# Five pieces of the conditioning weights are fetched in the opening stage, and ScalarE rounds the rows of the convolution

## The chip, the cores and the metric

The kernel runs on one core of one Trainium2 chip. The metric is the device time of one execution in microseconds (us), lower is better. It is one long program of about 137,000 instructions, written with explicit semaphores, one queue of instructions for each engine: TensorE (PE), VectorE (DVE), ScalarE (ACT), GpSimd (POOL) and SyncE (SP), which here only issues transfers.

## The reference, cut to what matters

One inference step of a network of four layers over 128 context tokens and 1024 latent tokens of 1024 channels, in float32. The mixers are RWKV-7, attention, a gated short convolution, and RWKV-7 again. Each layer is wrapped like this:

```python
def sublayer(x, cond, p, i, mixer_fn):
    ada = jax.nn.silu(cond) @ p['w_ada'][i] + p['b_ada'][i]     # 1024 -> 3072, two rows of cond
    shift, scale, gate = jnp.split(ada[:, None, :], 3, axis=-1)
    h = rmsnorm(x, p['norm_pre'][i]) * (1.0 + scale) + shift
    m, extra = mixer_fn(h)
    return x + gate * rmsnorm(m, p['norm_post'][i]), extra

def conv_mixer(h, p, j):
    proj = h @ p['conv_w_in'][j]                                # 1024 -> 4096
    bg, cg, u, g = jnp.split(proj, 4, axis=-1)
    ...
```

The change touches the product with `w_ada` (its fetching) and the rows `h` that enter `conv_w_in`.

## The kernel before

Activations lie in SBUF as 128 partitions (channels of a block) by 8 blocks by 1152 tokens. The scratch memory `arena` is four such arrays, `big[0]` to `big[3]`; `g.x` is a fifth. Tokens are worked in three chunks of 384, each a PSUM bank. The phases run one after the other and each ends in a barrier of all engines: opening, then for each layer projection, scan or attention, and a boundary with the output projection.

**Conditioning.** `w_ada` of the four layers is six groups of eight pieces, 1 MB each (128 partitions x 2048). A piece is multiplied with the two conditioning columns by `ada_products` (line 167). Group 0 is worked in the opening phase (`phase_open`, all eight pieces in `big[2]` and `big[3]`). Groups 1, 2 and 3, that is 24 pieces numbered 0 to 23, are worked in the projection phase of layer 0, and groups 4 and 5 in the convolution.

**Opening phase.** SP issues everything at once: x, ones, eight pieces, constants, and the first two weight slabs of the next phase. PE sums the squares, then takes the eight products (`rows_mm` counts the last). ACT copies four rows of the result, PE turns them, DVE has meanwhile scaled the eight blocks of x (line 305, `tmp_ok`), and then DVE and ACT apply scale and shift (lines 315 and 275). SP waits for its last transfers before the barrier.

**Projection phase of layer 0** (`phase_rwkv_project`). The 24 pieces pass through two buffers of 1 MB in `g.x[:, 4:8]`. PE runs `lora_down(0)`, `lora_down(1)` and `first_keys`, each of eight steps k = 0 to 7 of six fp32 matmul instructions (lines 588 and 626); behind each step `ada_between(n, k)` puts piece 2 + 8n + k, and pieces 0 and 1 come ahead of `lora_down(0)`. After the last step of `lora_down(0)` PE raises `proj_done` to 1, after that of `lora_down(1)` to 2, and only then comes the piece of k = 7. The rows of `lora_down(0)` are made in `big[2]` by ACT (line 798) and DVE (line 895), those of `lora_down(1)` in `big[3]`.

SP issues in program order and waits in that order too: `pieces(0, 12)`, then `slab(2)`, which waits for `proj_done` 1, then `pieces(12, 20)`, then `slab(3)`, which waits for `proj_done` 2, then `pieces(20, 24)`. A piece p of 2 or more waits until PE has used piece p - 2 (`piece_mm`).

When a group of eight is complete, ACT copies its rows out (line 183), PE turns them (`ada_columns`, behind step k = 2 of the next group of steps), and DVE adds the bias; DVE does that for group 1 behind its fifth row of the keys.

**Convolution** (`phase_conv`). Every matmul there is split in three with operands rounded to fp32r: high by high, high by low, low by high, in 32 slabs of 8 steps k of nine matmuls (line 370). DVE makes all operands: it rounds slab 0 (line 339) and subtracts (line 349), then for each of eight rows rounds (line 339) and subtracts (line 357), then does slab 1. PE's first slab waits for each row in turn. ACT loads a table at the start and has nothing to do until the first slab is done.

Of the kernel before, what the change touches and what calls it, by code (L numbers as in the profile page):

```python
# [22 lines left out]
NB = D // P  # L23
# [11 lines left out]
WSLOTS = 2  # L35
# [124 lines left out]
ADA_TILES = 4  # L160
# [3 lines left out]
def ada_products(pe, g, piece, bank, k):  # L164

    for t in range(ADA_TILES):
        mm = pe.matmul(g.ps[32 * t:32 * t + 2, bank, :], g.silu[:, 2 * k:2 * k + 2], piece[:, t * 512:(t + 1) * 512],
                       start=k == 0, stop=k == NB - 1)
    return mm
# [41 lines left out]
def phase_open(nc, g, layer):  # L211

    io = g.io
# [4 lines left out]
    size = ADA_TILES * 512  # L218
    pieces = [rest[:, k * size:(k + 1) * size] for k in range(NB)]
# [6 lines left out]
    with ExitStack() as ctx:  # L226
        sem = Sems(nc, ctx)
        cond_in, ident_in, ones_in, chan_in, next_in, set_ok, sig_ok, silu_ok = sem(
            "cond_in", "ident_in", "ones_in", "chan_in", "next_in", "set_ok", "sig_ok", "silu_ok")
# [7 lines left out]
        @block.sync  # L237
        def _(sp):
            sp.dma_start(cond, io["cond"]).then_inc(cond_in, 16)
            n = NB // X_PARTS  # L240
            for i in range(X_PARTS):
                sp.dma_start(g.x[:, n * i:n * i + n, :], io["x"][:, n * i:n * i + n, :]).then_inc(x_in[i], 16)
            sp.dma_start(g.ones[:, :], io["ones"]).then_inc(ones_in, 16)
            for k in range(NB):
                sp.dma_start(pieces[k], io["w_ada"][0, k]).then_inc(piece_in[k], 16)
            sp.dma_start(g.ident[:, :], io["ident"]).then_inc(ident_in, 16)
            sp.dma_start(g.chan[:, :], io["chan"]).then_inc(chan_in, 16)
            sp.dma_start(g.head_ones[:, :], io["head_ones"]).then_inc(next_in, 16)
            for s in range(WSLOTS):
                sp.dma_start(g.slab[:, s, :], io["w"][mixer_slabs(layer) + s]).then_inc(next_in, 16)  # L250
            sp.wait_ge(next_in, 16 * (WSLOTS + 1))

        @block.scalar
        def _(act):
# [82 lines left out]
def take_high(nc, dst, src):  # L337

    return nc.vector.tensor_copy(dst, src)
# [9 lines left out]
    nc.vector.tensor_tensor(g.slab_r[:, n % WSLOTS], g.slab[:, n % WSLOTS], g.stage_r[:, n % WSLOTS, 0:D], op=ALU.subtract).then_inc(low_ok, 1)  # L349


def split_rows(nc, g, dve, high, low, rows_high_ok, rows_ok):

    for k in range(NB):
        take_high(nc, g.big_r[high][:, k, :], g.big[low][:, k, :]).then_inc(rows_high_ok, 1)
        dve.wait_ge(rows_high_ok, k + 1)
        nc.vector.tensor_tensor(g.big_r[low][:, k, :], g.big[low][:, k, :], g.big_r[high][:, k, :], op=ALU.subtract).then_inc(rows_ok, 1)  # L357


def multiply_split(pe, g, high, low, slot, bank, done, rows_ok=None, late=None):  # L360

    w_high, w_low = g.stage_r[:, slot, 0:D], g.slab_r[:, slot]
# [36 lines left out]


ADA_WITH = ((1, 2, 3), (), (4, 5), ())


RWKV_MATS = (("decay", 4, 1), ("rate", 5, 1), ("key", 1, NB), ("receptance", 0, NB), ("value", 2, NB), ("gate", 3, NB))
# [2 lines left out]
def phase_rwkv_project(nc, g, layer, j):  # L407
# [17 lines left out]
    ada_in = ADA_WITH[layer]  # L425
# [31 lines left out]
    with ExitStack() as ctx:  # L457
# [19 lines left out]
        def _(sp):  # L477
# [49 lines left out]

            def pieces(first, last):
                for p in range(first, min(last, n_pieces)):
                    if p >= 2:  # L530
                        sp.wait_ge(piece_mm, p - 1)
                    sp.dma_start(piece[p % 2], g.io["w_ada"][ada_in[p // NB], p % NB]).then_inc(piece_in[p % 2], 16)

            pieces(0, 12)
            slab(2)
            pieces(12, 20)
            slab(3)
# [45 lines left out]
        def _(pe):  # L583
# [13 lines left out]
            def ada_piece(p):  # L597
                i = p // NB
                if p >= n_pieces:
                    return  # L600
                pe.wait_ge(piece_in[p % 2], 16 * (p // 2 + 1))
                if p % NB == 0 and i >= 2:
                    pe.wait_ge(cols_sb, i - 1)
                mm = ada_products(pe, g, piece[p % 2], ada_bank(i), p % NB)
                mm.then_inc(piece_mm, 1)

            def ada_columns(i):
# [3 lines left out]
                ada_turned(pe, g, ada_row[i % 2], ada_bank(i)).then_inc(cols_mm, 1)  # L611

            def ada_between(n, k):
                if n < 2 or k < 6:
                    ada_piece(2 + NB * n + k)
                if n and k == 2:
                    ada_columns(n - 1)

# [74 lines left out]
                bank_free(("sum", b, c))  # L693
                pe.matmul(g.ps[:, bank(("sum", b, c)), 0:CW], g.head_ones[:, :], prod[b % 2][:, chunk(c)], start=True, stop=True).then_inc(sum_mm, 1)

            ada_piece(0)
            ada_piece(1)
            lora_down(0)
            lora_down(1)
            first_keys()  # L700
# [20 lines left out]
        def _(act):  # L721
# [69 lines left out]
            def scaled_rows(m, k):  # L791
                r = RWKV_MATS[m][1]
                if m == 2:
                    if k < NB - 1:
                        act.wait_ge(rows_free, k + 1)
                    else:
                        act.wait_ge(proj_done, 2)
                A.activation((lora_xs[0], lora_xs[1], low)[m][:, k, :], h[:, k, :], ACT.Copy, scale=rest_mu[:, 8 * r + k:8 * r + k + 1]).then_inc(pre_ok, 1)

            def ada_row_copies(i):  # L800
# [73 lines left out]
        def _(dve):  # L874
# [116 lines left out]

            for b in range(NB):
                from_scaled(2, b, xs_ok)
                if b == 4:
                    ada_columns(0)
            high_slab_of(KEY + 1)
            for b in range(NB):
# [1279 lines left out]
def phase_conv(nc, g):  # L2277
# [11 lines left out]
    with ExitStack() as ctx:  # L2289
# [53 lines left out]

        @block.scalar
        def _(act):
            act.preload_act_table_set(SIGMOID)
            for b in range(NB):
                act.wait_ge(proj_done, 4 * b + 1)
                if b:
                    act.wait_ge(u_ok, b)  # L2350
                A.copy(as3(cs), slot_view(g.ps[:, 0:3, :])).then_inc(c_ok, 1)
                act.wait_ge(proj_done, 4 * b + 4)
                if b:
                    act.wait_ge(silu_ok, b)
                A.activation(as3(sig), slot_view(g.ps[:, 3:6, :]), ACT.Sigmoid).then_inc(sig_ok, 1)
                if b in (3, 5):
                    i = (b - 3) // 2
                    act.wait_ge(zero_ok, 1)
                    act.wait_ge(piece_mm, NB * (i + 1))
                    ada_rows(nc, g, ada_row[i], ada_bank(i), rows_sb)  # L2360
            act.preload_act_table_set(LN_EXP)

        @block.vector
        def _(dve):
            def next_slab(n):
                if n < 4 * NB:
                    split_slab(nc, g, dve, n, slab_in, proj_done, high_ok, low_ok)

            next_slab(0)
            split_rows(nc, g, dve, H_HIGH, H_LOW, rows_high_ok, rows_ok)  # L2370
            next_slab(1)
            for b in range(NB):
                dve.wait_ge(proj_done, 4 * b + 1)
                next_slab(4 * b + 2)
                w = lambda i: ch(g, "conv_w", 8 * i + b)
                dve.wait_ge(proj_done, 4 * b + 2)
                dve.wait_ge(c_ok, b + 1)
                V.tensor_tensor(as3(uu), slot_view(g.ps[:, 3:6, :]), as3(cs), op=ALU.mult).then_inc(evacuated, 1)
                next_slab(4 * b + 3)
                dve.wait_ge(evacuated, 3 * b + 1)  # L2380
                V.tensor_scalar(cv, uu, w(1), ch(g, "conv_b", b), ALU.mult, ALU.add).then_inc(w1_ok, 1)
                dve.wait_ge(w1_ok, b + 1)
                for _, a0, a1 in token_ranges():
                    V.scalar_tensor_tensor(cv[:, a0 + 1:a1], uu[:, a0:a1 - 1], w(0), cv[:, a0 + 1:a1], op0=ALU.mult, op1=ALU.add).then_inc(w0_ok, 1)
                dve.wait_ge(w0_ok, 2 * b + 2)
                for i, (_, a0, a1) in enumerate(token_ranges()):
                    V.scalar_tensor_tensor(cv[:, a0:a1 - 1], uu[:, a0 + 1:a1], w(2), cv[:, a0:a1 - 1], op0=ALU.mult, op1=ALU.add).then_inc(w2_ok, 1)
                dve.wait_ge(w2_ok, 2 * b + 2)
                V.tensor_copy(g.flag[:, 2:3], g.flag[:, 1:2]).then_inc(u_ok, 1)
                dve.wait_ge(proj_done, 4 * b + 3)  # L2390
                V.tensor_tensor(as3(cv), slot_view(g.ps[:, 0:3, :]), as3(cv), op=ALU.mult).then_inc(evacuated, 1)
                next_slab(4 * b + 4)
                dve.wait_ge(evacuated, 3 * b + 2)
                dve.wait_ge(sig_ok, b + 1)
                V.tensor_tensor(as3(gg), slot_view(g.ps[:, 3:6, :]), as3(sig), op=ALU.mult).then_inc(evacuated, 1)
                next_slab(4 * b + 5)
                dve.wait_ge(evacuated, 3 * b + 3)
                dve.wait_ge(u_ok, b + 1)
                V.tensor_tensor(og[:, b, :], cv, gg, op=ALU.mult).then_inc(silu_ok, 1)
                dve.wait_ge(silu_ok, b + 1)  # L2400
                if b in (4, 6):
                    i = b // 2 - 2
                    dve.wait_ge(cols_mm, i + 1)
                    ada_biased(nc, g, ada_in[i], ada_bank(i), cols_sb)
            dve.wait_ge(cols_sb, len(ada_in))
            ada_gate(nc, g, 2, vec_ok)
            ada_scale(nc, g, 3, vec_ok)
            ada_gate(nc, g, 3, vec_ok)
            dve.wait_ge(vec_ok, 3)
# [445 lines left out]
```

## Time and profile before

| | |
|---|---|
| time, median of 3 runs | 4689.62 us (4684.68 to 4690.49) |
| the profiled execution's own time | 4690.08 us |
| its span | 4688.3 us |
| PE, DVE, ACT busy | 91%, 58%, 40% |
| mean granted TensorE clock | 0.968 of full |

The span is the time from the first to the last instruction; a DMA issue, a wait and a branch are not counted as busy. SPq is the queue of SP, in which DMA issues stand. A wait that was released by an engine is shown behind the arrow in brackets.

### The profile page before, as it was taken

How to read it: one execution, taken by the hardware profiler on the slowest of the kernel's cores; microseconds unless marked ns; L12 is line 12 of the kernel's file. 1: busy time of each engine (PE TensorE's matmuls, PEld its weight loads, DVE VectorE, ACT ScalarE, POOL GpSimd, SP SyncE). 2: the span in 40 equal slices, each digit the busy share in tenths (PEclk: the TensorE clock that was granted, in tenths of full speed). 3: DMA queues.
4: the chain of work that ended last, by engine and by line, in shares of the span. 5: the costliest groups of instructions: out<-in, count | busy, mean ns of one | idle time of the engine just before them, and what ended most of it. 6: DMA issues, size and time to landing. Idle time of an engine off the chain costs nothing. (4 is left out here: it accounts for less than half of the span.)

```text
span 4688.3 us, 137401 instructions
## 1 busy us (share of the span) xinstructions
PE 4258.9 (91%) x61184; PEld 3665.6 (78%) x61184; DVE 2696.7 (58%) x4665; ACT 1887.8 (40%) x3496; POOL 4.6 (0%) x10
## 2 busy tenths in 40 slices
PE   6999979999997899999998999889999789999978
PEld 2888768888885799766668899877988678888858
DVE  5433547777775654355556433466425577777755
ACT  5333225545554432355554000154332245555542
POOL 0000000000000000000000000000000000000000
PEclk8999989999999999899999999999999899999989
DMA  7444773333325132100000221112446733333341
GB/s 294 150 123 123 223 225 87 98 83 97 87 80 192 63 84 56 51 1 2 1 10 28 95 95 68 57 52 82 117 139 195 236 110 89 98 85 96 85 183 63
DMA packets 542442, 480.77 MB, mean 103 GB/s; under 512 B 29344, under 2 KB 500640, under 8 KB 534176
## 3 DMA queue, kind: packets, MB, share of 16 engines
q1 hardware_dynamic: 411040, 405.91, 27.3%
q10 hardware_dynamic: 130816, 66.07, 5.2%
q8 instruction: 487, 7.98, 0.7%
q14 instruction: 99, 0.81, 0.1%
HBM read 337.94 MB, written 128.71 MB: 100 GB/s over the span
## 5 line engine op out<-in xcount | busy, mean ns | idle before, releaser
L647 PE MATMUL ps<-big_r,stage_r 128*128 128x384 f32 x2976 | 641.3, 350 | 19.1 <-DVE big_r L908 17.7
L647 PEld LDWEIGHTS ps<-big_r,stage_r 128*128 128x128 f32 x2976 | 522.6, 190 | 75.7 <-issue 27.0
L2508 PE MATMUL ps<-big_r,w_out 128*128 128x384 f32 x2304 | 417.8, 341 | 36.5 <-DVE w_out L2624 36.2
L2508 PEld LDWEIGHTS ps<-big_r,w_out 128*128 128x128 f32 x2304 | 407.7, 191 | 44.9 <-DVE w_out L2624 39.2
L647 PE MATMUL ps<-big_r,w_slab_r 128*128 128x384 f32 x1488 | 341.4, 337 | 0.0
L370 PE MATMUL ps<-big_r,stage_r 128*128 128x384 f32 x1536 | 311.7, 337 | 13.2 <-DVE big_r L357 13.2
L2230 DVE TENSOR_REDUCE extra<-ps 128x1 f32<-128x1152 f32 (+1 forms) x144 | 177.6, 1234 | 205.0 <-PE ps L2135 205.0
L370 PEld LDWEIGHTS ps<-big_r,stage_r 128*128 128x128 f32 x1536 | 270.7, 189 | 27.7 <-issue 26.7
L1491 ACT COPY arena<-ps 128x512 f32<-128x512 f32 x288 | 168.9, 587 | 253.4 <-PE ps L1294 252.9
L647 PEld LDWEIGHTS ps<-big_r,w_slab_r 128*128 128x128 f32 x1488 | 268.2, 189 | 0.0
L1645 DVE COPY_PREDICATED arena<-arena,ps 128x128 f32<-128x128 uint32 x720 | 192.9, 325 | 116.6 <-PE ps L1282 115.5
L1518 ACT COPY arena<-ps 128x256 f32<-128x256 f32 x360 | 136.4, 379 | 273.5 <-PE ps L1305 222.3
L764 ACT ACTIVATE x_resid<-ps,chan 128x384 f32<-128x384 f32 x192 | 101.1, 578 | 308.7 <-PE ps L685 224.4
L2156 PE MATMUL ps<-ident,arena 128*128 128x128 f32 x1168 | 189.4, 286 | 27.5 <-ACT arena L2215 20.9
L1282 PE MATMUL ps<-arena 64*64 64x32 f32 x7680 | 164.1, 222 | 55.1 <-ACT arena L1491 48.1
L1294 PE MATMUL ps<-arena 64*64 64x64 f32 x9216 | 202.5, 224 | 7.2 <-DVE arena L1645 2.5
L1247 PE MATMUL ps<-arena 64*128 64x128 f32 x2304 | 172.3, 289 | 38.7 <-DVE arena L1617 25.4
L1282 PEld LDWEIGHTS ps<-arena 64*64 64x64 f32 x7680 | 138.1, 135 | 77.8 <-ACT arena L1491 61.8
L1247 PEld LDWEIGHTS ps<-arena 64*128 64x128 f32 x2304 | 144.3, 191 | 67.9 <-issue 41.5
L1294 PEld LDWEIGHTS ps<-arena 64*64 64x64 f32 x9216 | 165.3, 135 | 39.1 <-issue 16.0
L1305 PE MATMUL ps<-ident,arena 128*128 128x128 f32 x1152 | 189.8, 287 | 3.5 <-issue 3.5
L2205 ACT ACTIVATE arena<-ps,extra 128x1152 f32<-128x1152 f32 (+1 forms) x144 | 162.1, 1126 | 74.1 <-DVE extra L2230 70.0
(259 smaller groups left out, 8087.5 us busy)
## 6 DMA issues: line engine op xcount, KB each, us to landing
w_slab<-in_w SPq DMA_DIRECT2D x138, 512.0 KB, 3.7
scan_in<-x_resid ACTq DMA_DIRECT2D x112, 576.0 KB, 5.9
arena<-scan_in SPq DMA_DIRECT2D x144, 320.0 KB, 3.8
arena<-scan_in SPq DMA_DIRECT2D x288, 128.0 KB, 3.8
arena<-scan_in SPq DMA_DIRECT2D x48, 576.0 KB, 7.5
arena<-scan_in SPq DMA_DIRECT2D x144, 192.0 KB, 4.0
arena<-in_w_ada SPq DMA_DIRECT2D x24, 1024.0 KB, 5.8
x_resid<-in_w_ada SPq DMA_DIRECT2D x24, 1024.0 KB, 4.9
```

What stands on the lines that cost most here:

```text
L370: mm = pe.matmul(g.ps[:, bank + c, 0:CW], w[:, k * P:(k + 1) * P], x[:, k, c * CW:(c + 1) * CW], start=k == i == 0, stop=k == NB - 1 and i ...
L647: mm = pe.matmul(g.ps[:, 3 * s + c, 0:CW], w[:, k * P:(k + 1) * P], x[:, k, chunk(c)], start=k == i == 0, stop=k == NB - 1 and i == 2)
L1247: mm = pe.matmul(strided(ps, (3 + h) * 512 + u * P, (1, P)), strided(bk[q % 2], u * 256 + t * P, (1, P), rows=HALVES[h]), strided(ar[q % 4 ...
L1282: mm = pe.matmul(strided(ps, p * 512 + u * 32, (1, 32), rows=HALVES[h]), strided(gr[q % 3], (1 - p) * 1024 + h * 512 + u * P, (1, HD), row ...
L1294: mm = pe.matmul(strided(ps, h * 512 + (2 * d + s) * HD, (1, HD), rows=HALVES[p]), strided(xt[q % 2], lx(d, p, s), (1, HD), rows=HALVES[h] ...
L1305: mm = pe.transpose(strided(ps, 2 * 512 + lx(d, 0, s), (P, 2), (1, HD)), strided(x, (2 * d + s) * P, (1, P)), g.ident[:, :])
L1491: A.copy(strided(x, 0, (HD, 2), (P, 4), (1, HD)), strided(ps, 0, (512, 2), (HD, 4), (1, HD))).then_inc(xa_ok, 1)
L1645: V.copy_predicated(strided(wk(k), p * P, (256 + n, 2), (2 * n, HD // n), (1, n)), bits(strided(level_mask, (k - 1) * P, (HD, 2), (n, HD / ...
L2156: mm = pe.transpose(g.ps[:, bank, i * P:(i + 1) * P], prob[n % 2][h][:, (3 * k + i) * P:(3 * k + i + 1) * P], g.ident[:, :])
L2205: A.activation(prob[n % 2][h][:, 0:width(n)], scored(n, h), ACT.Exp, bias=nmax[n % 2][h], accum_out=rsum[n % 2][h]).then_inc(exp_ok, 1)
L2230: V.tensor_reduce(nmax[n % 2][h], scored(n, h), mybir.AxisListType.X, ALU.max, negate=True).then_inc(max_ok, 1)
L2508: mm = pe.matmul(g.ps[:, bank(i, b), 0:wide[i]], w[:, b, k * P:(k + 1) * P], r, start=k == j == 0, stop=k == NB - 1 and j == 2)
```

## The change

Five of the 24 pieces are now issued in the opening phase: pieces 2, 3 and 4 into `big[3]` once its eight products are done, pieces 0 and 1 into `g.x[:, 4:8]` once the blocks of x there have been scaled. The opening phase ends when they have landed. The projection phase multiplies them ahead of `lora_down(0)`; the pieces between the steps are now numbered 5 + 8n + k, without the bound on n and k. The lists that SP walks become `pieces(5, 12)`, `slab(2)`, `pieces(12, 20)`, `slab(3)`, `pieces(20, 24)`, and the wait of each is counted from the two buffers anew. ACT waits for the five products before it writes rows of `lora_down(1)` into `big[3]`. DVE takes the columns of group 1 behind its second row of the keys and not its fifth. In the convolution ACT rounds the eight rows ahead of its table load, and DVE only subtracts. The last layer's projection has no pieces and keeps its order.

```diff
@@ phase_open, sync
-            sp.wait_ge(next_in, 16 * (WSLOTS + 1))
+            sp.wait_ge(rows_mm, 1)
+            for p in range(2, ADA_EARLY):
+                sp.dma_start(early_piece(g, p), io["w_ada"][ADA_WITH[layer][0], p]).then_inc(next_in, 16)
+            for p in range(2):
+                sp.wait_ge(tmp_ok, (6, NB)[p])
+                sp.dma_start(early_piece(g, p), io["w_ada"][ADA_WITH[layer][0], p]).then_inc(next_in, 16)
+            sp.wait_ge(next_in, 16 * (WSLOTS + 1 + ADA_EARLY))
@@
+ADA_EARLY = 5
+def early_piece(g, p):
+    size = ADA_TILES * 512
+    if p < 2:
+        return g.x[:, 4:8, :].rearrange("p b t -> p (b t)")[:, p * size:(p + 1) * size]
+    return g.big[3].rearrange("p b t -> p (b t)")[:, (p - 2) * size:(p - 1) * size]
@@ phase_rwkv_project, sync
             def pieces(first, last):
                 for p in range(first, min(last, n_pieces)):
-                    if p >= 2:
-                        sp.wait_ge(piece_mm, p - 1)
-                    sp.dma_start(piece[p % 2], g.io["w_ada"][ada_in[p // NB], p % NB]).then_inc(piece_in[p % 2], 16)
-            pieces(0, 12)
+                    i = p - ADA_EARLY
+                    sp.wait_ge(piece_mm, i + 1 if i < 2 else p - 1)
+                    sp.dma_start(piece[i % 2], g.io["w_ada"][ada_in[p // NB], p % NB]).then_inc(piece_in[i % 2], 16)
+            pieces(ADA_EARLY, 12)
             slab(2)
             pieces(12, 20)
             slab(3)
@@ phase_rwkv_project, tensor
-                pe.wait_ge(piece_in[p % 2], 16 * (p // 2 + 1))
+                r = p - ADA_EARLY
+                if r >= 0:
+                    pe.wait_ge(piece_in[r % 2], 16 * (r // 2 + 1))
...
-                mm = ada_products(pe, g, piece[p % 2], ada_bank(i), p % NB)
+                mm = ada_products(pe, g, piece[r % 2] if r >= 0 else early_piece(g, p), ada_bank(i), p % NB)
...
             def ada_between(n, k):
-                if n < 2 or k < 6:
-                    ada_piece(2 + NB * n + k)
+                ada_piece(ADA_EARLY + NB * n + k)
...
-            ada_piece(0)
-            ada_piece(1)
+            for p in range(ADA_EARLY):
+                ada_piece(p)
@@ phase_rwkv_project, scalar
+                if m == 1 and k == 0 and ada_in:
+                    act.wait_ge(piece_mm, ADA_EARLY)
@@ phase_rwkv_project, vector
-                if b == 4:
+                if b == 1:
                     ada_columns(0)
@@ phase_conv, scalar
+            for k in range(NB):
+                A.copy(g.big_r[H_HIGH][:, k, :], g.big[H_LOW][:, k, :]).then_inc(rows_high_ok, 1)
             act.preload_act_table_set(SIGMOID)
@@ phase_conv, vector
-            split_rows(nc, g, dve, H_HIGH, H_LOW, rows_high_ok, rows_ok)
+            for k in range(NB):
+                dve.wait_ge(rows_high_ok, k + 1)
+                V.tensor_tensor(g.big_r[H_LOW][:, k, :], g.big[H_LOW][:, k, :], g.big_r[H_HIGH][:, k, :], op=ALU.subtract).then_inc(rows_ok, 1)
```

## Rows read from the trace of the kernel before

**Rows 1.** The page, its first part: busy us, share, instructions of each engine.

```profile
PE 4258.9 (91%) x61184; PEld 3665.6 (78%) x61184; DVE 2696.7 (58%) x4665; ACT 1887.8 (40%) x3496; POOL 4.6 (0%) x10
```

**Rows 2.** Timeline of the opening phase: start, duration, engine, line.

```profile
33.40 7.05 PE L167 MATMUL ps<-arena,silu 128*2 128x512 f32 x64
37.29 10.24 DVE L305 TENSOR_TENSOR arena<-x_resid,extra 128x1152 f32<-128x1152 f32 x8 [2.42 <-ACT extra L267]
47.88 6.17 ACT L275 ACTIVATE arena<-arena,ada 128x128 f32<-128x128 f32 x8 [4.93 <-DVE ada L200]
55.10 17.71 SPq L532 DMA_DIRECT2D x_resid<-in_w_ada  x6
```

**Rows 3.** Timeline of the projection phase's start, all engines.

```profile
56.64 18.45 ACT L798 ACTIVATE arena<-arena,stage 128x1152 f32<-128x1152 f32 x16
58.04 1.42 DVE L895 SCALAR_TENSOR_TENSOR arena<-arena,stage 128x1152 f32<-128x1152 f32 x1 [0.46 <-ACT arena L798]
60.01 1.89 PE L167 MATMUL ps<-x_resid,silu 128*2 128x512 f32 x8 [16.29 <-DMA x_resid<-in_w_ada]
64.30 4.05 PE L588 MATMUL ps<-arena,w_slab 128*128 128x384 f32 x6
68.28 1.04 PE L167 MATMUL ps<-x_resid,silu 128*2 128x512 f32 x8
69.25 2.20 PE L588 MATMUL ps<-arena,w_slab 128*128 128x384 f32 x6
71.38 1.04 PE L167 MATMUL ps<-x_resid,silu 128*2 128x512 f32 x8
```

**Rows 4.** Waits between 64 and 142 us: total, times, longest.

```profile
PE ps L167 <- DMA x_resid<-in_w_ada: 2.5, 5, 0.6
```

**Rows 5.** Waits of SP's queue from 55 to 145 us.

```profile
SPq L532 <- PE ps L167: 67.9, 22, 6.0
```

**Rows 6.** Timeline of SP at slab(2), and of PE at the first split slab.

```profile
88.00 4.15 SPq L532 DMA_DIRECT2D x_resid<-in_w_ada  x2
92.19 0.43 SPq L485 DMA_DIRECT2D w_slab<-in_w  x1
141.75 1.50 PE L647 MATMUL ps<-big_r,stage_r 128*128 128x384 f32 x6
```

**Rows 7.** Line 532's transfers; then those issued from 91 to 101 us, median to landing.

```profile
DMA to landing us min/median/max: 4.7/4.9/7.0
w_slab<-in_w SPq DMA_DIRECT2D x1, 512.0 KB, 5.9
```

**Rows 8.** Windows: us, PE, PEld, DVE, ACT, POOL busy (instructions), PEclk, DMA, GB/s.

```profile
24.00:27.00 3.00, 3.00 (x11) 1.81 (x10) 0.00 (x0) 2.22 (x2) 0.00 (x0) 1.00 1.02 423
47.60:54.00 6.40, 0.00 (x0) 0.00 (x0) 4.22 (x10) 6.12 (x8) 0.00 (x0) 0.50 0.00 0
2563.30:2570.00 6.70, 4.25 (x7) 2.31 (x8) 6.53 (x13) 4.49 (x8) 0.00 (x0) 0.50 0.00 0
2587.70:2593.80 6.10, 6.07 (x19) 6.10 (x20) 6.00 (x7) 0.00 (x0) 0.00 (x0) 0.50 0.00 0
```

**Rows 9.** Timeline of PE before the convolution: a wait inside the boundary phase.

```profile
2565.75 8.79 PE L2536 MATMUL ps<-arena,ones 128*128 128x384 f32 x16 [6.16 <-ACT arena L2573]
```

**Rows 10.** Timeline of the convolution's start.

```profile
2585.44 0.75 DVE L339 CAST big_r<-arena 128x1152 fp32r<-128x1152 f32 x1
2586.23 1.36 DVE L357 TENSOR_TENSOR big_r<-arena,big_r 128x1152 fp32r<-128x1152 f32 x1
2587.73 2.26 PE L370 MATMUL ps<-big_r,stage_r 128*128 128x384 f32 x6 [13.19 <-DVE big_r L357]
2604.46 1.20 PE L370 MATMUL ps<-big_r,stage_r 128*128 128x384 f32 x6
2606.02 1.20 PE L370 MATMUL ps<-big_r,stage_r 128*128 128x384 f32 x6
```

**Rows 11.** Line 724: ACT's rounding of a row; duration ns min/median/max.

```profile
L724 ACT CAST big_r<-arena x64: 1134/1155/1167, 98.2 to 3563.0; 128x1152 fp32r<-128x1152 f32 x64
```

More of the change, by code:

```diff
@@ L349, in split_slab @@
     nc.vector.tensor_tensor(g.slab_r[:, n % WSLOTS], g.slab[:, n % WSLOTS], g.stage_r[:, n % WSLOTS, 0:D], op=ALU.subtract).then_inc(low_ok, 1)
[L352 to L357, printed above, removed]
 def multiply_split(pe, g, high, low, slot, bank, done, rows_ok=None, late=None):
```

## The prediction

> **What bounds the kernel now.** I read the page first: PE is busy 91% of the span [rows 1], so an edit counts only where it changes when PE works. The change touches two stretches, and each was read in the timeline, then in the waits. In the opening, the eight products end at 40.45 (33.40 + 7.05), DVE's scaling of x ends at 47.53, ACT's last shift at 54.05, and the next phase begins at 55.10 [rows 2]. PE has no work until the first piece, issued at 55.10, lands at 60.01, and `lora_down(0)` starts at 64.30 [rows 3]. From there to 141.75, where the first split slab starts [rows 6], PE is the bound: it waits 2.5 us in all for pieces, in 5 waits [rows 4], while SP is the one that waits for PE, 67.9 us in 22 waits [rows 5]. One step costs 2.13 us (69.25 to 71.38), and one piece 0.97 us (68.28 to 69.25) [rows 3]. In the convolution PE's first slab starts when DVE's first row is ready, 2587.73 [rows 10].
>
> **The pieces fetched ahead: when the opening ends.** Between 47.6 and 54 no transfer runs [rows 8], so the fetch lies beside other work, but it is 5 MB in a short time. A piece alone takes 4.9 us from issue to landing [rows 7]. The full stream is 423 GB/s [rows 8], by which 1.05 MB takes 2.5 us; the other 2.4 us are fixed. SP is released at 40.5 for three pieces. Pieces 0 and 1 are released after six and eight of DVE's scalings (10.24 / 8 = 1.28 us each), at 45.0 and 47.5, while earlier ones still stream. So the fifth lands at 40.6 + 2.4 + 5 x 2.5 = 55.5, against ACT's end at 54.05 today: SP becomes the last one at the barrier and the next phase starts 1.4 us later, at 56.5. Bounds: 0, if the stream is as fast as the cover allows, and 2.8 if each of the last two takes 0.7 longer. I take 1.4.
>
> **The start of the projection phase.** PE now has five pieces at once. The clock stands at 0.50 (1.2 GHz) in the idle stretch. After PE resumed elsewhere it stayed there for 4.3 us (2565.75 to 2570.0) [rows 8, 9] and 6.1 us (2587.7 to 2593.8) [rows 8], and here for some 8 us, with gaps between the products (60.01 to about 68.2, where the short groups begin) [rows 3]. For unbroken work I take 5.2, between the first two. A piece at the slow clock costs 1.75 us (twice 7.05 / 8 = 0.88, and 1.89 for one alone). In 5.2 us go three pieces, two more take 1.8: `lora_down(0)` starts at 56.5 + 7.0 = 63.5, 0.8 us before today. Its first step no longer runs slow (4.05 against 2.20 [rows 3]), 1.9 us more. Gain 2.7, the later start paid. Bounds: 3.2, if the clock rises after 4.3 us; -1.6, if products with two columns of weights don't raise it (five slow pieces end at 65.2, then 5.2 us of steps run slow and lose 2.6, against 1.9 today).
>
> **The steps.** Three pieces fewer lie between the steps: 3 x 0.97 = 2.9 us. Of the 2.5 us of small waits [rows 4] I leave 0.5, gain 2.0 (0 to 2.5). DVE's first row is ready at 59.46 today, so about 60.9, ahead of 63.5. ACT's new wait for five products costs nothing: it comes to `lora_down(1)`'s rows half way through its 18.45 us, at 67 [rows 3], with PE done at 63.5. DVE's columns behind its second row: the piece that needs them is now that behind step 3 of `lora_down(1)`, one step (2.13 us) after the turn; the add of some 0.2 us fits. Were it left behind the fifth row, the engines would block each other. Together these stretches give 2.7 + 2.9 + 2.0 = 7.6 us.
>
> **What SP's order does to the shifted pieces.** This is the step that decides. Behind step k = 7 of `lora_down(0)` stood piece 9; now piece 12 stands there. But SP issues `pieces(5, 12)`, then `slab(2)`, then piece 12, and `slab(2)` waits for `proj_done` 1, which PE raises with that very step 7. Today piece 12 has until k = 2 of `lora_down(1)`. Now PE comes to it at once, with its transfer not yet issued, though its buffer was free since step 5. The same holds for piece 20, behind step 7 of `lora_down(1)`, and `slab(3)`. How long: today piece 11 is issued at about 91.8 (the last of the two issues that end at 92.15) and the slab at 92.19, and the slab lands 5.9 us later, so 1.5 MB takes 6.3 us from the first issue [rows 6, 7]; slab and piece in the other order are the same 1.5 MB. I take 6.3 for each stall, 12.6 for both. Bounds for one: 5.3 (a lone piece's 4.9 and the slab's issue of 0.43) and 8.8 (piece 13, issued behind it, streams beside it and ends first, 2.5 more). Behind PE nothing else is late: rows, ACT's copies and slabs get longer cover.
>
> **The clock after a stall.** In the boundary phase PE waited 6.16 us, and worked at 0.50 after it until 2570 [rows 8, 9]. So each stall should be followed by about 5.2 us of work at 1.2 GHz, of which half is lost: 2.6 each, 5.2 for both. Bounds: 0 and 6.2. The Trainium skill (TensorE: Matmul & The Clock Gate, "HAM oscillation — how this bites in real kernels") warns of this: when matmuls wait for a transfer between groups, the clock falls back and the next group starts cold. By that rule the two stalls cost 17.8 us, without it 12.6. The trace agrees with the rule where it shows a 6.16 us wait.
>
> Sum in this stretch: 12.6 + 5.2 - 7.6 = +10.2 us, and PE stays the bound behind 141.75, so all of it passes on.
>
> **The convolution.** DVE's roundings go (0.75 each), ACT's take 1.155 [rows 11], start at the phase's start and run ahead of DVE, whose subtractions come each 1.3 us behind slab 0. The first row is ready 0.79 us sooner (2585.44 against 2586.23). After that the rows of today hardly hold PE up: it takes 16.73 us for the slab (2587.73 to 2604.46) [rows 10], and its own work is 6.1 us at the slow clock (two steps, at twice the 1.56 us from 2604.46 to 2606.02), six steps at 1.56 and one piece of 0.97, together 16.4 to 16.5 [rows 8, 10]. So 0.2 us of small waits go too. ACT's table load moves behind its roundings, which end 8 x 1.155 = 9.2 us after the phase's start, and nothing asks for ACT before PE's first slab ends, 21.7 us after it. Gain 1.0, bounds 0.4 (the clock rises no sooner, so half of 0.79 is given back, and no wait goes) and 1.3.
>
> Total: +9.2 us on the profiled execution's own 4690.08, which stands 0.5 above the median: 4699.
>
> **Rivals.** (A) The clock doesn't fall in the stalls. Then 12.6 - 7.6 - 1.0 = +4.0, 4694. For it: a stall of 6.3 us has one match in the rows, and the place of that one is another phase. Against it: that one match ran at 0.50 behind the wait [rows 8, 9]. (B) Not slower: the fetched pieces give SP its lead and PE finds piece 12 and 20 ready, so that the gains alone stand: -7.6 - 1.0 = -8.6, 4681.5. It holds if the slab's wait is over before PE reaches step 7's piece; the change is no loss from a stall of (7.6 + 1.0) / 2 = 4.3 us each downwards if the clock holds, and from 4.3 - 2.6 = 1.7 us if it falls. For it speaks that SP is ahead of PE today. Against it: the release of the slab is the end of the step directly before the piece, and the 2.4 us of a transfer that are no streaming can't be hidden behind anything there. The Trainium skill (DMA: Bandwidth & Descriptors, "Rules for kernel authors") says to issue early and wait late, so that the fixed cost overlaps; by it the change would be all gain. The same page ("Anatomy of one DMA") says that a semaphore wait is done by the issuing sequencer ahead of dispatch, by which what is behind the slab's wait isn't early. (C) Stalls near their upper bound, with piece 13 in the same stream, or products that don't raise the clock: 2 x 1.5 more, or 4.3 more: 4702 to 4703.
>
> **How the numbers follow.** My forecast 0.68 (its own range 4695 to 4702), A 0.10, B 0.05, C 0.17. A difference under 0.2%, 9.4 us, can't be told from none here. The forecast lies at that bound, +9.2. I give a little under half of it, and nearly all of C, to slower; A and the rest of the forecast to no change; B sits at the edge of faster. Faster 0.04, same 0.48, slower 0.48. The range reaches into A and C, with both ends of the clock's cost: 4691 to 4704.
>
> **What would show it.** In the trace after: the last instruction of the opening waits for SP and the next phase starts at about 56.5; `lora_down(0)` starts at 63 to 64; two waits of PE on `in_w_ada` of about 6.3 us, right behind the last steps of `lora_down(0)` (near 87) and `lora_down(1)` (near 121), with the slab's issue at their start; a clock of 0.50 behind each; the first split slab at about 152. In the convolution PE starts 4.2 us after the phase and not 5.0. I am wrong if PE's longest wait for a piece stays under 2 us, or if the clock holds at 1.00 through both, or if the opening's end moves by over 3 us.

## The result, and the profile after

The changed kernel takes 4700.34 us (median of 12 runs, 4687.86 to 4707.96) against 4690.18 of before on the same chip. Ratio 1.0021, 95% interval 1.0012 to 1.0029: slower by 0.21%, or 9.8 us (the two medians are 10.2 apart). One of the 12 runs of before took 13653.26 us, and the ratio leaves it out. The prediction was 4699. The profiled execution spans 4698.2 us, 9.9 more than before.

The timeline of PE and SP in the opening and the projection phase of the changed kernel, in order of time (start, duration, engine, line; line 253 and 256 are the fetches, 539 the other pieces, 492 the slabs, 595 and 634 the steps, 655 the split slabs):

```profile
40.73 1.28 SPq L253 DMA_DIRECT2D arena<-in_w_ada  x3
45.24 2.86 SPq L256 DMA_DIRECT2D x_resid<-in_w_ada  x2
48.09 6.17 ACT L281 ACTIVATE arena<-arena,ada 128x128 f32<-128x128 f32 x8 [4.93 <-DVE ada L200]
56.61 3.60 PE L167 MATMUL ps<-x_resid,silu 128*2 128x512 f32 x16 [12.67 <-PEq L151]
59.97 3.53 PE L167 MATMUL ps<-arena,silu 128*2 128x512 f32 x24
63.44 2.20 PE L595 MATMUL ps<-arena,w_slab 128*128 128x384 f32 x6
65.57 1.04 PE L167 MATMUL ps<-x_resid,silu 128*2 128x512 f32 x8
...
85.84 2.20 PE L595 MATMUL ps<-arena,w_slab 128*128 128x384 f32 x6
88.07 0.33 SPq L492 DMA_DIRECT2D w_slab<-in_w  x1
88.44 25.45 SPq L539 DMA_DIRECT2D x_resid<-in_w_ada  x8
94.23 1.88 PE L167 MATMUL ps<-x_resid,silu 128*2 128x512 f32 x8 [6.19 <-DMA x_resid<-in_w_ada]
96.05 3.69 PE L595 MATMUL ps<-arena,w_slab 128*128 128x384 f32 x6
...
122.56 0.33 SPq L492 DMA_DIRECT2D w_slab<-in_w  x1
128.59 1.88 PE L167 MATMUL ps<-x_resid,silu 128*2 128x512 f32 x8 [6.06 <-DMA x_resid<-in_w_ada]
130.41 3.58 PE L634 MATMUL ps<-arena,w_slab 128*128 128x384 f32 x6
...
150.97 1.50 PE L655 MATMUL ps<-big_r,stage_r 128*128 128x384 f32 x6
```

Read it against [rows 2, 3, 6]. ACT ends the opening's work at 54.26, and the next phase starts at 56.6 and not 55.1. `lora_down(0)` starts at 63.44, 0.86 us sooner than before and at the fast clock. Then come the two stalls, each with the slab's issue at its start: the last step of `lora_down(0)` ends at 88.0, SP issues the slab at 88.07 and piece 12 at 88.44, and PE has it at 94.23 (the slab itself landed 3.6 us after its issue, at 91.7). The second stall is the same, from 122.53 to 128.59. The first split slab starts at 150.97 against 141.75: +9.22 us.

SP's own waits from 55 to 152 us in the changed kernel (what waited, for whom: total, times, longest) show its waits ahead of the slabs, for the last step, and what held the end of the opening:

```profile
SPq L492 <- PE ps L595: 17.2, 2, 8.6
SPq L226 <- DMA x_resid<-in_w_ada: 7.4, 1, 7.4
```

And the windows of the changed kernel (columns as in [rows 8]) show the clock in the first products, and ahead of, in and behind the stalls:

```profile
56.70:61.00 4.30, 4.30 (x24) 0.78 (x23) 3.80 (x6) 4.29 (x6) 0.82 (x1) 0.50 0.34 86
61.40:61.80 0.40, 0.40 (x8) 0.10 (x4) 0.40 (x1) 0.40 (x2) 0.00 (x0) 0.83 1.01 430
88.10:91.80 3.70, 0.00 (x0) 0.00 (x0) 2.98 (x3) 1.11 (x1) 0.00 (x0) 1.00 0.76 270
92.00:92.50 0.50, 0.00 (x0) 0.00 (x0) 0.00 (x0) 0.00 (x0) 0.00 (x0) 0.76 0.83 344
92.00:98.50 6.50, 4.27 (x12) 1.62 (x13) 0.00 (x0) 0.00 (x0) 0.00 (x0) 0.52 0.72 281
99.00:99.20 0.20, 0.20 (x1) 0.10 (x1) 0.00 (x0) 0.00 (x0) 0.00 (x0) 0.79 1.16 492
126.00:132.60 6.60, 4.01 (x12) 1.39 (x13) 1.92 (x2) 3.78 (x6) 0.00 (x0) 0.53 0.80 300
```

A value between 0.50 (1.2 GHz) and 1.00 (2.4 GHz) means that the change lies within the window. In the products the clock rose at about 61.6. It fell within the first stall, at about 92.2, and rose again at about 99.1, so that PE worked at 1.2 GHz for 4.8 us behind it (94.23 to 99.1). In the second stall it fell at about 126.4, and PE worked slowly for 4.6 us.

In the convolution (phase start at 2593.17), the rows answering to [rows 10, 11]:

```profile
2593.18 8.54 ACT L2357 CAST big_r<-arena 128x1152 fp32r<-128x1152 f32 x8 [1.01 <-PEq L151]
2595.84 10.23 DVE L2384 TENSOR_TENSOR big_r<-arena,big_r 128x1152 fp32r<-128x1152 f32 x8
2597.34 2.26 PE L368 MATMUL ps<-big_r,stage_r 128*128 128x384 f32 x6 [12.39 <-DVE big_r L2384]
2612.80 1.20 PE L368 MATMUL ps<-big_r,stage_r 128*128 128x384 f32 x6
```

The clock rises there at about 2601.05, 3.7 us after PE's first matmul (6.2 in the kernel before):

```profile
2600.90:2601.30 0.40, 0.40 (x3) 0.40 (x3) 0.40 (x2) 0.40 (x1) 0.00 (x0) 0.81 0.00 0
```

PE starts 4.17 us after the phase (4.96 before), and its second slab 19.63 us after it (21.69 before, 2604.46 - 2582.77): 2.06 us won, where 1.0 was forecast.

### The profile page after: what moved, and what is told of

Same layout as the page of the kernel before. It is cut to its first block and busy times, and to the rows that moved or that the text cites. A ratio compares the mean times of both kernels' runs of the same rounds, so it can differ in the third digit from the quotient of the medians.

```text
span 4698.2 us, 137401 instructions
## 1 busy us (share of the span) xinstructions
PE 4261.7 (91%) x61184; PEld 3666.5 (78%) x61184; DVE 2690.5 (57%) x4657; ACT 1895.6 (40%) x3504; POOL 4.6 (0%) x10
```

## The experiments

In all of them "first split slab" is the start of the first of the split slabs, the end of the stretch that the change touches. Two executions with the same code up to there, in which the clock rises at the same place, agree there to 0.6 us (141.75 in the kernel before, 141.12 in the kernel with the convolution's part alone); a rise at another place was worth 1.9 us in one of those below. Whole runs of one kernel differ by 14 to 25 us.

**SP's order.** The slabs are moved behind three more pieces:

```diff
-            pieces(ADA_EARLY, 12)
+            pieces(ADA_EARLY, 15)
             slab(2)
-            pieces(12, 20)
+            pieces(15, 23)
             slab(3)
-            pieces(20, 24)
+            pieces(23, 24)
```

> The changed kernel with SP's lists as pieces(5, 15), slab(2), pieces(15, 23), slab(3), pieces(23, 24): piece 12 and piece 20 no longer stand behind a slab that waits for the step just ahead of them. My theory (the order behind the slabs costs two stalls of 6.2 and 6.1 us and the slow clock after them 2.5 us each, 17 us in all): both stalls go, small waits of about 1 us come back, the clock stays at 1.00, the first split slab starts at about 135 us and not 150.97, the time is 16 us under the changed kernel's and 7 under that of before, ratio to before 0.9985. Rival (the transfers themselves are late, since five fetched pieces move the stream closer to its limit): the waits go to other pieces, the first split slab stays near 148 to 151, ratio 1.001 to 1.002.

Measured: ratio 0.9984 (0.9974 to 0.9993). PE's waits for pieces are small again; these are the three over 0.2 us and the first split slab:

```profile
97.54 1.04 PE L167 MATMUL ps<-x_resid,silu 128*2 128x512 f32 x8 [0.32 <-DMA x_resid<-in_w_ada]
110.81 1.04 PE L167 MATMUL ps<-x_resid,silu 128*2 128x512 f32 x8 [0.21 <-DMA x_resid<-in_w_ada]
123.72 1.04 PE L167 MATMUL ps<-x_resid,silu 128*2 128x512 f32 x8 [0.42 <-DMA x_resid<-in_w_ada]
134.56 1.50 PE L655 MATMUL ps<-big_r,stage_r 128*128 128x384 f32 x6
```

16.4 us sooner than in the changed kernel (150.97), with the same transfers, bytes and instructions. The change of order alone turns +9.8 us into about -7.5 (interval of the ratio: -12 to -3). The rival, transfers that are late by themselves, is out: the waits that come back are 1.2 us in 4 waits.

**Stall and clock apart.** Eight matmuls that nobody reads are put ahead of PE's wait for pieces 12 and 20 (for piece 20 they wait until ACT has copied the bank out):

```diff
+                if p in (12, 20):
+                    if p == 20:
+                        pe.wait_ge(copied, 1)
+                    for _ in range(8):
+                        pe.matmul(g.ps[:, 3 if p == 12 else 0, 0:CW], g.ones[:, :], g.chan[:, 0:CW], start=True, stop=True)
```

> The changed kernel, with eight matmuls more (ones by constants, into a PSUM bank that nobody reads before it is started anew) ahead of PE's wait for piece 12 and for piece 20: 5.7 us of work inside each stall. It does 16 matmuls that the result doesn't need. My theory (stall and clock are two costs): the transfers land as before, the waits that are left are about 0.5 us, the clock stays at 1.00, and the first split slab starts 4.9 us sooner, at 146. Ratio to before about 1.001. Rival (the steps behind the stalls are slow for another reason, or the clock falls all the same): first split slab at 151, ratio 1.002.

Measured: ratio 1.0011 (1.0001 to 1.0022). PE around piece 12, and the first split slab:

```profile
88.73 5.32 PE L613 MATMUL ps<-chan,ones 128*128 128x384 f32 x16
94.95 1.04 PE L167 MATMUL ps<-x_resid,silu 128*2 128x512 f32 x8 [0.90 <-DMA x_resid<-in_w_ada]
95.92 2.20 PE L595 MATMUL ps<-arena,w_slab 128*128 128x384 f32 x6
146.75 1.50 PE L660 MATMUL ps<-big_r,stage_r 128*128 128x384 f32 x6
```

The step behind the piece takes 2.20 us and not 3.69. In this execution the projection phase began 0.9 us later, so from its first product (57.50) to the first split slab it is 89.25 us, against 94.36 (150.97 - 56.61): 5.1 us less. The piece and the step behind each stall now take 3.10 us, against 5.44 and 5.32: 4.6 of the 5.1 us are the clock, and PE got them back by doing more work. The rest is other small waits for pieces, 0.8 less, and a start that took 0.2 longer. The waits that are left behind the added matmuls are 0.90 and 1.07 us, where 0.5 was forecast, and 146.75 is 0.75 behind the forecast, about as much as the late start. The whole-time ratios of this one and the changed kernel overlap; the trace decides it.

**The order alone, in the kernel before.**

```diff
-            pieces(0, 12)
+            pieces(0, 9)
             slab(2)
-            pieces(12, 20)
+            pieces(9, 17)
             slab(3)
-            pieces(20, 24)
+            pieces(17, 24)
```

> The kernel before, with one thing of the changed one: SP's lists are pieces(0, 9), slab(2), pieces(9, 17), slab(3), pieces(17, 24), so that the piece behind the last step of lora_down(0) and of lora_down(1) is issued behind a slab that waits for that step. Nothing is fetched ahead. My theory: two stalls of 6.2 us and 2.5 us of slow clock behind each, less about 1.7 of the small waits of before (those of the pieces beside the slabs); the first split slab starts at 141.75 + 15.5 = 157, ratio to before 1.0033. Rival (in the kernel before there is slack in SP's order that takes it up): under 5 us.

Measured: ratio 1.0032 (1.0020 to 1.0044). Its two stalls, the step behind the first, and its first split slab:

```profile
94.96 1.88 PE L167 MATMUL ps<-x_resid,silu 128*2 128x512 f32 x8 [6.22 <-DMA x_resid<-in_w_ada]
96.77 2.99 PE L588 MATMUL ps<-arena,w_slab 128*128 128x384 f32 x6
128.12 1.89 PE L167 MATMUL ps<-x_resid,silu 128*2 128x512 f32 x8 [6.25 <-DMA x_resid<-in_w_ada]
153.90 1.50 PE L647 MATMUL ps<-big_r,stage_r 128*128 128x384 f32 x6
```

The same stalls with nothing fetched ahead. The first split slab came 12.2 us later, not 15.5; in this execution the clock had risen by the first step (64.36, 2.20 us and not 4.05), which is 1.9 of the 3.3 us missing. Most of the rest is in the rows too: the slow clock behind the stalls cost 1.6 us (94.96 to 99.69, against 3.10) and 2.1 (128.12 to 133.34), 3.7 in all where 5.0 was forecast, and of the 2.5 us of small waits only 0.3 are left, where 0.8 was forecast.

**Two pieces ahead and not five** (`ADA_EARLY = 2`, the lists as they are, so that the numbering and the order of the kernel before come back).

> The changed kernel with two pieces fetched in the opening and not five (those in x, none in the scratch memory); SP's lists are pieces(2, 12), slab(2), pieces(12, 20), slab(3), pieces(20, 24), as in the kernel before, and the pieces between the steps are numbered as there. My theory: the fetch lands by 52.5 us, ahead of ACT's end at 54, so the next phase starts at 55.1; PE takes two pieces at the slow clock to 58.7, waits for DVE's first row at 59.5, and starts lora_down(0) at 59.6, the first step or two at the slow clock; no stall behind the slabs. The first split slab starts 3 to 5 us sooner than before, at 137 to 139; ratio to before 0.999. Rival (fetching ahead gives nothing since DVE's rows bound the start of lora_down(0)): DVE makes a row each 2.8 us against PE's 3.1, so that under 1 us is won.

Measured: ratio 0.9985 (0.9975 to 0.9995), first split slab at 138.42. The start:

```profile
55.26 3.59 PE L167 MATMUL ps<-x_resid,silu 128*2 128x512 f32 x16 [11.37 <-PEq L151]
59.63 4.21 PE L595 MATMUL ps<-arena,w_slab 128*128 128x384 f32 x6 [0.78 <-DVE arena L905]
```

The barrier isn't later, PE waits 0.78 us for DVE's first row, and the first step runs at the slow clock (4.21 us against 2.20). Of the 4.7 us by which it starts sooner, 3.3 arrive; of the difference, 0.9 are small waits for pieces (3.4 us in 6 waits, against 2.5 in 5). Whole times of this and the kernel with the moved order can't be told apart, though the first split slab is 3.9 us apart.

**Four pieces ahead, moved order** (`ADA_EARLY = 4`; `pieces(4, 14)`, `slab(2)`, `pieces(14, 22)`, `slab(3)`, `pieces(22, 24)`).

> The kernel with the moved order, and four pieces fetched in the opening and not five; SP's lists are pieces(4, 14), slab(2), pieces(14, 22), slab(3), pieces(22, 24). My theory (the fifth piece's landing, and nothing else, held the opening's end): the four land by 53, the next phase starts at 55.1 to 55.3 and not 56.6, lora_down(0) at 61.5 to 62.5, one piece more lies between the steps, and the first split slab starts 0.5 to 1.5 us sooner than with five, at 133 to 134. Ratio to before 0.998. Rival (the barrier is late for another reason, such as pieces 0 and 1 being released late by VectorE): the phase starts at 56.6 again, and the first split slab at 135.5.

Measured: ratio 0.9985 (0.9976 to 0.9994), the phase starts at 55.44, `lora_down(0)` at 60.39, the first split slab at 132.63, 1.9 us sooner than with five. So the landing of the fifth piece did hold the barrier. The four landed at about 54.3 and not by 53, just ahead of ACT's end at 54.4. `lora_down(0)` and the first split slab were earlier than I expected (61.5 to 62.5, and 133 to 134), since the clock rose while the products ran: two took 3.27 us, the next two 1.89. The rise came 2.8 us after the first product, against 5.0 with five pieces. PE does half as much at the slow clock, so by my estimate half of that difference, 1.1 of the 1.9 us, is the clock's, so what four pieces win over five is nearer to 0.8 us.

```profile
55.48 3.27 PE L167 MATMUL ps<-x_resid,silu 128*2 128x512 f32 x16 [11.41 <-PEq L151]
58.57 1.89 PE L167 MATMUL ps<-arena,silu 128*2 128x512 f32 x16
60.39 0.91 PE L595 MATMUL ps<-arena,w_slab 128*128 128x384 f32 x2
```

**The convolution alone**, the kernel before with the convolution's part of the diff.

> The kernel before with the convolution's part of the change alone: ScalarE rounds the eight rows, VectorE subtracts. My theory: PE starts its first slab 4.2 us after the phase's start and not 5.0, and finishes it 1.0 us sooner if the clock takes as long to rise, that is 20.6 to 20.8 us after the phase's start against 21.69 in the kernel before; the 19.63 of the changed kernel had the clock rise 3.3 us after PE's start against 6.1. Ratio to before 0.9998, not to be told from 1. Rival (the shorter row time itself gives the 2 us): 19.6 us after the phase's start with the clock rising as late as before.

Measured: ratio 0.9999 (0.9990 to 1.0008), not to be told from 1, as expected. PE starts 4.17 us after the phase; the second slab comes 19.69 us after it, better than the 20.6 to 20.8 forecast for a late rise, but the clock rose early here too, 3.8 us after PE's start. The rival (the shorter rows give the 2 us by themselves, with a late rise too) fails on the kernel with four pieces ahead, where the rise was late and the second slab came at 20.71. What shows the rest is the old split with an early rise, which the third experiment (the order alone) happens to hold. Its convolution starts at 2592.43, its PE at 2597.39, and the clock rises 3 us later. Its windows, with one of the kernel with four pieces ahead at the end:

```profile
2597.40:2600.30 2.90, 2.90 (x9) 2.90 (x10) 2.83 (x4) 0.00 (x0) 0.00 (x0) 0.50 0.00 0
2600.50:2612.00 11.50, 10.87 (x63) 9.10 (x61) 11.33 (x12) 0.00 (x0) 0.00 (x0) 1.00 0.01 1
2580.50:2580.90 0.40, 0.40 (x3) 0.40 (x3) 0.40 (x2) 0.00 (x0) 0.00 (x0) 0.70 0.00 0
```

And its steps, in order of time:

```profile
2605.55 1.33 PE L370 MATMUL ps<-big_r,stage_r 128*128 128x384 f32 x6 [0.20 <-DVE big_r L357]
2607.62 1.31 PE L370 MATMUL ps<-big_r,stage_r 128*128 128x384 f32 x6 [0.20 <-DVE big_r L357]
2609.68 1.32 PE L370 MATMUL ps<-big_r,stage_r 128*128 128x384 f32 x6 [0.23 <-DVE big_r L357]
2614.12 1.20 PE L370 MATMUL ps<-big_r,stage_r 128*128 128x384 f32 x6
```

PE now stands 2.07 us apart from step to step, which is the pace of DVE's rounding and subtracting, and the second slab starts 21.69 us after the phase, the same as with the late rise. The table (us; the rise from PE's first matmul, the second slab from the phase's start):

| execution | rows made by | clock rises after PE's start | second slab |
|---|---|---|---|
| before | DVE | 6.2 | 21.69 |
| order alone | DVE | 3.0 | 21.69 |
| four ahead | ACT and DVE | 6.1 | 20.71 |
| convolution alone | ACT and DVE | 3.8 | 19.69 |
| changed kernel | ACT and DVE | 3.7 | 19.63 |
| order moved, kept warm, two ahead | ACT and DVE | 3.5 to 3.6 | 19.56 to 19.60 |

The expectation has 3.3 for the changed kernel; the window above gives 3.7. So the new split is worth 1.0 us with a late rise and 2.0 with an early one. In the old one DVE's pace holds PE as soon as the clock is up, and an earlier rise bought nothing.

**Clock kept up at both starts.** The kernel with four pieces ahead, with matmuls that nobody reads (14 behind the turn in the opening, 3 ahead of the convolution's first slab):

```diff
             ada_turned(pe, g, rows, COLS).then_inc(cols_mm, 1)
+            pe.wait_ge(chan_in, 16)
+            for _ in range(14):
+                pe.matmul(g.ps[:, 5, 0:CW], g.ones[:, :], g.chan[:, 0:CW], start=True, stop=True)
...
+            for _ in range(3):
+                pe.matmul(g.ps[:, 7, 0:CW], g.ones[:, :], g.chan[:, 0:CW], start=True, stop=True)
             for b in range(NB):
                 block_of(b, b == 0)
```

> The kernel with four pieces ahead and the moved order, with 14 matmuls that nobody reads behind the turn in the opening, and 3 ahead of the convolution's first slab (both into banks that are started anew), to keep or raise the clock while PE has nothing to do. They are no part of the computation. My theory: the clock is at 1.00 when the projection phase starts, its four pieces take 3.6 us, PE then waits for VectorE's first row at 59.5, and lora_down(0) starts at 59.6 at the fast clock, 2 us sooner than without; the steps then take 3.1 us each against VectorE's row each 2.8, so it holds: first split slab at about 131.5. In the convolution PE's clock rises at most 3 us after its first slab starts; 0 to 1.5 us. Ratio to before 0.9975. Rival (VectorE's rows bound these steps): first split slab at 133 or later.

Measured: ratio 0.9980 (0.9971 to 0.9989), the best of all, but not to be told from the other three (0.9984, 0.9985, 0.9985). The projection phase's products do run fast, and then:

```profile
57.62 1.90 PE L167 MATMUL ps<-arena,silu 128*2 128x512 f32 x16
60.29 0.91 PE L598 MATMUL ps<-arena,w_slab 128*128 128x384 f32 x2 [0.77 <-DVE arena L908]
132.34 1.51 PE L658 MATMUL ps<-big_r,stage_r 128*128 128x384 f32 x6
```

The forecast missed here: 132.34 and not 131.5. The miss lies ahead of the steps. SP's wait for its transfers was 6.9 us, against 6.1 in the kernel with four pieces, and the phase began at 55.87 and not at 55.44. DVE's first row, for which the forecast had PE wait too, came later with it, and `lora_down(0)` starts at 60.29 and not 59.6. From there to the first split slab it is 72.05 us, and 71.9 was forecast. PE waits for a row this once (0.77 us), so the rival, that VectorE's rows bound the steps, fails as well. The clock kept up is worth 0.7 us from the first product to the first split slab (76.43 us, against 77.15 with four pieces alone), of which 0.3 arrive. Why the transfers took longer is open. In the convolution the second slab comes 18.21 us after the phase (2589.94 - 2571.73), 1.4 us sooner than the best without (19.56).

## Why the prediction was right

By its own steps, with the size predicted and the size measured:

- **The opening's end**, +1.4: the phase starts 1.5 us later, after SP's wait of 7.4 us for its transfers. The stream of five was the last to end, and with four it no longer was.
- **Start of `lora_down(0)`**, 63.5: 63.44. The products alone do raise the clock: it stood at 0.50 from 56.7 to 61.0, with nothing but products on PE, rose at 61.6, 5.0 us after the first of them (5.2 was taken), and the last three took 3.53 us. The lower bound of that term is out.
- **The steps.** 2.9 us for three pieces was short. A step that no piece follows takes 1.88 us and not 2.13 (in the changed kernel five of them run from 141.58 to 150.97), so a piece between two steps costs 1.2 us and three are worth 3.7. Small waits were 1.1 us (13.3 in 4 waits, less the two long ones), not 0.5.
- **The stalls**, 6.3 each: 6.19 and 6.06. Undoing the order takes them away, and putting the order into the kernel before makes them: this cause is shown from both sides.
- **The clock behind a stall**, 2.6 us each: it fell both times. Behind the first the piece and the step took 1.82 and 3.62 us (starts at 94.23, 96.05, 99.67) for 0.97 and 2.13, a loss of 2.3; behind the second 2.2. Keeping PE busy gave both back. The trace agrees with the rule quoted from the Trainium skill (TensorE: Matmul & The Clock Gate, "HAM oscillation — how this bites in real kernels"), that a wait for a transfer between groups of matmuls lets the clock fall and the next group start slow.
- **Sum in this stretch**, +10.2: +9.22. The measured terms give -0.86 (start) - 1.85 (first step no longer slow) - 3.7 - 1.4 (small waits 2.5 to 1.1) + 12.25 + 4.5 = +8.9; 0.3 us are not accounted for. Two errors nearly offset each other here: the pieces between the steps were worth 0.8 us more than forecast, and the small waits 0.6 less. The stalls and the slow clock cost 1.0 less.
- **The convolution**, -1.0: -2.06 in the profiled execution. This term was mis-sized for it. I took the clock's rise as fixed at the late one and worked out PE's waits from that; with an early rise the old rows are the bound. At a late rise 1.0 was right (20.71 against 21.69). Of the six executions with the new split and no matmuls ahead, five had the early rise.
- **The whole.** +9.22 - 2.06 is +7.2 us, and the profiled spans differ by 9.9. The convolution phase starts 10.4 us later, so 1.2 came in between, and 1.6 more behind. No code there differs, no experiment was made on it, and it is within what executions of one kernel differ by: from the order-moved kernel to that with four pieces, the first split slab moves by 1.9 us and the convolution's start by 12.8. The forecast of the total was thus nearer than its terms deserve.

Rival A (the clock holds) failed with the two windows at 0.52 and 0.53. Rival B (not slower) failed as the kernel stood, but it is what the moved order gives: -8.6 was forecast for it, ratio 0.9984 is -7.5. Rival C (longer stalls, or products that don't raise the clock) failed too: piece 13 was issued right behind piece 12, and piece 12 still landed 5.8 us after its issue. C's own sum was too low by the bounds given: 8.8 for one stall is 2.5 above 6.3 and not 1.5, which makes 4704 and not 4702. The prefetch advice of the Trainium skill (DMA: Bandwidth & Descriptors, "Rules for kernel authors") says to issue early; in the changed kernel the fetches were early and the time went up by 9.8 us, and only with the list reordered did it go down, by 7.5.

## What to carry to other kernels

When a prefetch shifts which item is consumed where, walk the issuing queue's list again: every wait on it must be over early enough for the item behind it to land before its consumer comes to it. Five transfers fetched ahead won about 7 us (134.56 against 141.75), and two that stood too far back in SP's list lost 16. A stall of 6 us in TensorE's stream cost 1.6 to 2.3 us more in the clock behind it here, so price both, and take away the engine that is late next (here VectorE's first row) before paying to keep the clock up.

## What the runs showed of the hardware

With the slab (0.5 MB) issued at 88.07 and piece 12 (1 MB) at 88.44, the slab landed after 3.6 us and the piece after 5.8 (94.23). With the piece first, the slab behind it took 5.9 us from its own issue [rows 7]. The five fetched pieces, 5 MB issued from 40.73 on, were all there by about 55.6 (the last took 7.8 us from its issue at about 47.8). PE ran nothing but products with two columns of weights from 56.61 on, and the granted clock rose from 0.50 to 1.00 (2.4 GHz) at 61.6. In the convolution the rise came 3.0 and 6.2 us after PE's first matmul in two executions with the old split, and 3.5 to 6.1 us in six with the new one. These are different kernels, but their code in that place is the same, so the delay differed from execution to execution; whether it does within one kernel isn't shown, since each profile is of one execution.
